# Eight of twelve groups of a modulation product moved from TensorE in the preparing stage to GpSimd in the gated linear stage

## The chip, the cores and the metric

The kernel runs on one core of one Trainium2 chip. The metric is the device time of one execution in microseconds (us). The engines are named as in the profile: PE (TensorE matmul) and PEld (its weight loads), DVE (VectorE), ACT (ScalarE), POOL (GpSimd), and SP (SyncE), which here only issues DMAs. Each engine works through its own instructions in their order, and waits on semaphores for the others.

## The reference, cut to what matters

The program is a mixer with two branches, a mixture of experts, and a second model of two layers. Only the modulation is touched. `c` and `c_ctx` are vectors of 1024, `w_mod` is 1024 x 6144, and each of the six parts is 1024 wide:

```python
mod_lat = split(silu(c) @ w_mod + b_mod, 6)         # sh1, sc1, g1, sh2, sc2, g2
mod_ctx = split(silu(c_ctx) @ w_mod + b_mod, 6)     # only csh1, csc1 are used: need_ctx is false
h_lat = rms_norm(x, norm_mix_g) * (1 + sc1) + sh1   # before the mixer
h_ctx = rms_norm(ctx, norm_mix_g) * (1 + csc1) + csh1
x = x + g1 * token_mixer(h_lat, h_ctx)              # delta-rule branch, gated linear branch, merge
h = rms_norm(x, norm_ffn_g) * (1 + sc2) + sh2       # before the experts
x = x + g2 * moe_ffn(h)
```

So `sh1` and `sc1` are wanted for both vectors before the mixer, and `g1, sh2, sc2, g2` for `c` alone, from the end of the merge on. All data are float32.

## The kernel before

The code is written out engine by engine, in stages (`stage`, line 156) that end with a barrier of all engines. `build` calls `prepare`, `gdn` (the delta-rule branch, 134.9 to 700 us), `gla` (the gated linear branch), `merge`, `experts` and `second`, each a row of such stages.

**prepare** computes the modulation and the first norm. The 6144 columns go in 12 groups of 512, each a 2 MB load (`load_group`) into one of four slots. Per group, PE multiplies `cs` (silu of both vectors, two columns) with the group's eight row tiles (L505), DVE copies the 2 x 512 result out of its bank (L522), PE turns it to columns with four small matmuls one group later (L495), and DVE adds the bias into `modT` (L526). `modT` has 48 columns of 128 for each vector: 0 to 15 are `sh1, sc1` (groups 0 to 3), 16 to 47 the other four parts (groups 4 to 11). In between DVE makes the inverse root (L545), scales the tokens (L550, behind group 3), makes `gain` (L553, L555, in group 4) and writes `hT` in eight steps of two instructions (L533, in groups 5 to 8). The stage ends with the last L526. The next stage reads `hT` and `wba`.

**gla** has a first stage, in which SP issues the weights `wh` of heads 0 and 1 (`load_head`, 3 MB each) and PE makes the low-rank gate (L1232), and a main stage (L1248 on) with four heads. Head 0 is projected alone: PE runs `project(0, 0..7)`, `inside(0)`, `project(0, 8)`, and DVE `decay(0, 0..7)`. Then for each head there are eight steps `i`. In step `i` PE makes the state update (L1340), for `i >= 4` the outputs (L1352, L1354), and `project(h + 1, i)`; DVE makes `state(h, i)` (L1462, L1470) and then `decay(h + 1, i)`, and parts of `norm(h - 1)`. What PE takes from DVE in the order of the program:

- the outputs of step `i` wait for `state(h, i - 1)`, which stands on DVE behind `decay(h + 1, i - 2)`;
- `project(h + 1, 7)` waits for `value(h + 1, 0)` (L1450), the end of `decay` part 5;
- `inside(h + 1)` (L1308, L1313) waits for the third product (L1436) of part 6 for each direction.

Most of the DVE instructions of `decay` read two tensors in SBUF: L1378, L1393, the two scans L1401, L1407, L1410, six subtractions L1422 to L1424, eight products L1436; L1380, L1387 and L1395 read and write SBUF with one tensor. `state` and the copies L1384, L1389, L1450 read one operand in PSUM. SP issues head `h + 2` when both matmuls of part 7 and 8 of head `h` are done (`rb_mm`, L1261). POOL has no instruction in `gla`. PE's last work there is `squares(3)` (L1321), DVE's the last part of `norm(3)` (to L1498). **merge** reads columns 16 to 23 of `modT` at L1674.

## Time and profile before

| | us |
|---|---|
| median of 3 runs | 3244.03 (3236.37 to 3245.56) |
| the profiled execution, device time | 3235.3 |
| its span, first to last instruction | 3233.5 |
| PE busy in the span | 3010.9 (93%) |
| DVE busy | 2097.6 (65%) |
| ACT busy | 1608.9 (50%) |
| POOL busy | 143.7 (4%) |
| second part of prepare (L505 on) | about 27.7 to 134.9 |
| main stage of gla | 723.6 to 969.7 |

Device time and span differ by 1.8 us. A time in a row is counted from the start of the span. A matmul of float32 leaves two records on PE and two on PEld, so `x64` in a row of PE is 32 matmuls. In the diff and in the order rows, the line numbers of the changed kernel are its own.

### The profile page before, as it was taken

The page shows a single profiled execution, that of the slowest core. Times are in us where ns is not written, and L with a number is a line of the kernel's source. Part 1 is how long each engine was busy: PE and PEld are TensorE (multiplying, and loading weights), DVE is VectorE, ACT ScalarE, POOL GpSimd, SP SyncE. Part 2 cuts the span into 40 slices and gives each one's busy share as a digit, 9 for nine tenths or more (in the row PEclk, how much of TensorE's full clock was granted, in tenths as well). Part 3 has the DMA queues.
Part 4 walks back from the last instruction along what each step waited for, and adds up shares of the span by engine and source line. Part 5 has one row for each costly group of instructions (what it writes and reads, how often), then busy time and mean ns, then how long its engine had stood idle before and what let it go on. Part 6 is the DMA issues. An engine that isn't in the chain of part 4 may idle for free. (4 is left out here: it accounts for less than half of the span.)

```text
span 3233.5 us, 44597 instructions
## 1 busy us (share of the span) xinstructions
PE 3010.9 (93%) x17512; PEld 2454.1 (76%) x17513; DVE 2097.6 (65%) x3195; ACT 1608.9 (50%) x2237; POOL 143.7 (4%) x175
## 2 busy tenths in 40 slices
PE   7989999989989789999999999999697899997998
PEld 2458888857669767777777777777595799986998
DVE  2135555535546578998998998998474556574665
ACT  0024444422215277777777777776332435442453
POOL 0022233200000000000000000000000000000000
PEclk9899999999979889999999999999795799995999
DMA  7551110021106579999999999996450255540453
GB/s 263 157 93 28 33 40 7 1 81 39 40 1 200 179 297 361 364 357 362 365 358 360 365 363 355 363 368 241 136 146 11 60 166 174 150 124 1 137 183 124
DMA packets 257563, 602.58 MB, mean 186 GB/s; under 512 B 25954, under 2 KB 82505, under 8 KB 257225
## 3 DMA queue, kind: packets, MB, share of 16 engines
q1 hardware_dynamic: 256268, 599.25, 54.2%
q8 instruction: 142, 2.33, 0.3%
q14 instruction: 68, 0.56, 0.1%
q10 hardware_dynamic: 1085, 0.45, 0.1%
HBM read 595.24 MB, written 4.39 MB: 185 GB/s over the span
## 5 line engine op out<-in xcount | busy, mean ns | idle before, releaser
L2000 DVE TENSOR_TENSOR moe_raw_r<-moe_raw,moe_hi 128x2048 fp32r<-128x2048 f32 x320 | 720.6, 2286 | 36.9 <-ACT moe_hi L1939 36.9
L1939 ACT ACTIVATE moe_hi<-moe_raw 128x2048 fp32r<-128x2048 f32 x320 | 599.3, 1906 | 0.0
L2722 PE MATMUL banks<-xs_r,w_hi 128*128 128x272 f32 (+1 forms) x1632 | 475.5, 291 | 25.2 <-DVE w_raw_r L3144 16.6
L2726 PE MATMUL banks<-xs_r,w_raw_r 128*128 128x272 f32 (+1 forms) x1632 | 472.8, 290 | 0.0
L2723 PE MATMUL banks<-xs_r,w_hi 128*128 128x272 f32 (+1 forms) x1632 | 470.2, 288 | 0.0
L1835 PE MATMUL banks<-moe_raw_r,moe_xs 128*128 128x512 f32 x1024 | 387.1, 435 | 0.0
L2966 ACT ACTIVATE w_hi<-w_raw 128x512 fp32r<-128x512 f32 (+1 forms) x416 | 256.9, 619 | 245.2 <-PE banks L2726 202.2
L2722 PEld LDWEIGHTS banks<-xs_r,w_hi 128*128 128x128 f32 x1632 | 311.3, 191 | 30.4 <-issue 22.4
L2726 PEld LDWEIGHTS banks<-xs_r,w_raw_r 128*128 128x128 f32 x1632 | 311.3, 191 | 2.9
L2723 PEld LDWEIGHTS banks<-xs_r,w_hi 128*128 128x128 f32 x1632 | 311.8, 191 | 0.2
L3144 DVE TENSOR_TENSOR w_raw_r<-w_raw,w_hi 128x512 fp32r<-128x512 f32 (+1 forms) x416 | 271.5, 676 | 56.9 <-ACT w_hi L2966 52.8
L1835 PE MATMUL banks<-moe_hi,moe_xs 128*128 128x512 f32 x772 | 296.4, 439 | 12.3 <-DVE moe_raw_r L2000 10.5
L1835 PEld LDWEIGHTS banks<-moe_raw_r,moe_xs 128*128 128x128 f32 x1024 | 193.8, 189 | 34.4
L1871 PEld LDWEIGHTS banks<-con,gu_tok 128*128 128x128 f32 x1024 | 190.9, 191 | 28.9 <-ACT gu_tok L1947 8.6
L791 PE MATMUL banks<-hT,wq 128*128 128x256 f32 (+1 forms) x512 | 180.3, 495 | 4.1 <-PEq L163 1.6
L1835 PE MATMUL banks<-moe_hi,y_tok_r 128*128 128x512 f32 x508 | 170.8, 418 | 5.3 <-DVE gu L2010 3.0
L1835 PEld LDWEIGHTS banks<-moe_hi,moe_xs 128*128 128x128 f32 x772 | 141.4, 190 | 45.2 <-issue 23.6
L1871 PE MATMUL banks<-con,gu_tok 128*128 128x64 f32 x1024 | 170.1, 250 | 1.1 <-ACT gu_tok L1947 1.1
L1835 PE MATMUL banks<-moe_raw_r,y_tok_r 128*128 128x512 f32 x512 | 162.0, 398 | 0.0
L2000 DVE TENSOR_TENSOR moe_raw_r<-moe_raw,moe_yT_r 128x2048 fp32r<-128x2048 f32 x64 | 146.3, 2286 | 0.0
L1050 DVE COPY_PREDICATED Tt<-gcon,banks 128x512 f32<-128x512 uint32 x112 | 81.1, 732 | 93.1 <-PE banks L838 68.1
L1880 PE MATMUL banks<-y_tok,pickT 128*128 128x512 f32 x256 | 139.7, 631 | 1.2 <-ACT y_tok L1958 1.2
(474 smaller groups left out, 5305.1 us busy)
## 6 DMA issues: line engine op xcount, KB each, us to landing
moe_raw<-in_w_gu SPq DMA_DIRECT2D x256, 1024.0 KB, 8.2
moe_raw<-in_w_down SPq DMA_DIRECT2D x128, 1024.0 KB, 10.2
w_raw<-in_w_ff SPq DMA_DIRECT2D x256, 256.0 KB, 3.0
w_raw<-in_w_in SPq DMA_DIRECT2D x112, 256.0 KB, 2.7
ring_mod<-in_w_mod SPq DMA_DIRECT2D x12, 2048.0 KB, 8.2
wq<-in_w_in SPq DMA_DIRECT2D x32, 512.0 KB, 4.3
wh<-in_w_in SPq DMA_DIRECT2D x8, 1024.0 KB, 9.5
mg_raw<-in_w_in SPq DMA_DIRECT2D x32, 256.0 KB, 3.0
```

What stands on the lines that cost most here:

```text
L791: ins = pe.matmul(out, wq[:, h % 2, n, k, :], hT[:, k, lo:TOK], start=(k == 0), stop=(k == KT - 1))
L1050: dve.copy_predicated(Tt[:, d, :, :], level_mask(d, lv), tiled(ps[4 + d][:, :])).then_inc(tt_v, 1)
L1835: ins = pe.matmul(ps[pair(e) + c][:, :], x[:, k, :], w[:, k * D + c * 512:k * D + c * 512 + 512], start=(q == 0 and i < 2), stop=(q == 3 a ...
L1871: ins = pe.matmul(ps[pair(e) + h][:, i * SLOTS:(i + 1) * SLOTS], gs[:, s, (4 * h + m) * P:(4 * h + m + 1) * P], fold, start=True, stop=True)
L1880: ins = pe.matmul(ps[4 + i][:, :], pickTs[e % 2][:, t * P:(t + 1) * P], y[:, c * 512:(c + 1) * 512], start=False, stop=(e == NEXP - 1))
L1939: act.activation(hi[n % HI_SLOTS][:, :], raw[n % UNITS][:, :], ACT.Copy).then_inc(his, 1)
L2000: dve.tensor_tensor(rest[n % UNITS][:, :], raw[n % UNITS][:, :], hi[n % HI_SLOTS][:, :].bitcast(F32), ALU.subtract).then_inc(los, 1)
L2722: pe.matmul(bank, w_hi, x[:, 0, 0:n_cols], start=first, stop=False)
L2723: pe.matmul(bank, w_hi, x[:, 1, 0:n_cols], start=False, stop=False)
L2726: ins = pe.matmul(bank, w_lo, x[:, 0, 0:n_cols], start=False, stop=last)
L2966: act.activation(hi[n % HI2][:, 0:w], raw[n % RING2][:, 0:w], ACT.Copy).then_inc(his, 1)
L3144: dve.tensor_tensor(rest[n % RING2][:, 0:w], raw[n % RING2][:, 0:w], hi[n % HI2][:, 0:w].bitcast(F32), ALU.subtract).then_inc(los, 1)
```

## The change

`prepare` keeps groups 0 to 3 and drops groups 4 to 11, with their loads, matmuls, turns and copies. DVE makes `gain` and all of `hT` at the end of the stage. `cs` now lives for the whole program.

`gla` gets the eight dropped groups, for `c` alone. A group is loaded in two halves of four row tiles (`load_mod`, 1 MB, 16 units in all) into two slots. POOL multiplies a half with the four columns of `cs` (128 x 2048), adds its two pairs (128 x 1024), and adds again (128 x 512); the second half has one more addition, to the first half's sum. That is 7 instructions for a group and 56 in all, each of which waits for the one before it. PE sums over the partitions at the stage's end with 32 matmuls of one column against `ones`, and one DVE instruction adds the bias. SP issues units 0 and 1 behind `wh` in the first stage; units 2 to 4 ahead of head 2, units 5 to 8 behind head 2, units 9 to 15 behind head 3, each when POOL is through with the unit two before it.

```diff
             @block.sync
             def _(sp):
-                for g in range(4, 12):
-                    sp.wait_ge(summed, g - 3)
-                    load_group(sp, g)
...
-                for g in range(12):
-                    pe.wait_ge(mod_in[g % 4], g // 4 * 16 + 16)
-                    if g >= 4:
-                        pe.wait_ge(copied, g - 3)
+                for g in range(4):
+                    pe.wait_ge(mod_in[g], 16)
...
-                    if g == 4:
-                        dve.wait_ge(taken, 4)
-                        dve.tensor_scalar(gain[:, :, :], modT[:, KT:2 * KT, :], 1.0, None, ALU.add).then_inc(gained, 1)
...
-                    if 5 <= g <= 8:
-                        shifted(2 * g - 10)
-                        shifted(2 * g - 9)
-                group_out(11)
+                group_out(3)
+                dve.wait_ge(taken, 4)
+                dve.tensor_scalar(gain[:, :, :], modT[:, KT:2 * KT, :], 1.0, None, ALU.add).then_inc(gained, 1)
...
+                for k in range(KT):
+                    shifted(k)
...
+        def load_mod(sp, u):
+            g, half = 4 + u // 2, u % 2
+            sp.dma_start(mod_ring[:, half], a["w_mod"][0][half * 4 * P:(half + 1) * 4 * P, g * 512:(g + 1) * 512]
+                         .rearrange("(k p) n -> p k n", p=P)).then_inc(mod_in[half], 16)
...
             @block.sync
             def _(sp):
+                def late(*units):
+                    for u in units:
+                        sp.wait_ge(mod_p, 7 * (u // 2 - 1) + (3, 7)[u % 2])
+                        load_mod(sp, u)
+
+                late(2, 3, 4)
                 for h in range(GLA_H - 2):
                     sp.wait_ge(rb_mm, 2 * h + 2)
                     load_head(sp, h + 2)
+                    late(*range(5 + 4 * h, 9 + 4 * h))
+                late(13, 14, 15)
+
+            @block.gpsimd
+            def _(pool):
+                for g in range(8):
+                    for half in range(2):
+                        w, n = mod_ring[:, half], 7 * g + 3 * half
+                        pool.wait_ge(mod_in[half], g * 16 + 16)
+                        pool.tensor_tensor(w, w, cs[:, 4 * half:4 * half + 4, 0:1].broadcast_to([P, 4, 512]), ALU.mult).then_inc(mod_p, 1)
+                        pool.wait_ge(mod_p, n + 1)
+                        pool.tensor_tensor(w[:, 0:2, :], w[:, 0:2, :], w[:, 2:4, :], ALU.add).then_inc(mod_p, 1)
+                        pool.wait_ge(mod_p, n + 2)
+                        if half == 0:
+                            pool.tensor_tensor(mod_sum[:, g, :], w[:, 0, :], w[:, 1, :], ALU.add).then_inc(mod_p, 1)
+                        else:
+                            pool.tensor_tensor(w[:, 0, :], w[:, 0, :], w[:, 1, :], ALU.add).then_inc(mod_p, 1)
+                            pool.wait_ge(mod_p, n + 3)
+                            pool.tensor_tensor(mod_sum[:, g, :], mod_sum[:, g, :], w[:, 0, :], ALU.add).then_inc(mod_p, 1)
...
                 squares(GLA_H - 1)
+                pe.wait_ge(mod_p, 7 * 8)
+                for m in range(4 * 8):
+                    ins = pe.matmul(ps[2][:, m:m + 1], mod_sum[:, m // 4, m % 4 * P:(m % 4 + 1) * P], ones[:, 0:1],
+                                    start=True, stop=True)
+                ins.then_inc(mod_mm, 1)
...
                 for part in range(3):
                     norm(GLA_H - 1, part)
+                dve.wait_ge(mod_mm, 1)
+                dve.tensor_tensor(modT[:, 2 * KT:6 * KT, 0], ps[2][:, 0:4 * KT], vec[:, V_BMOD + 2 * KT:V_BMOD + 6 * KT], ALU.add)
```

DVE in the second part of prepare, before, from the scaling of the tokens on:

```order
L550 TENSOR_TENSOR allT<-allT,rinv 128x512 x8
L522 COPY rows_mod<-banks 2x512
L526 TENSOR_TENSOR modT<-banks,vec 128x8
L553 TENSOR_SCALAR gain<-modT 128x16
L555 TENSOR_TENSOR gain<-gain,vec 128x16
L522 COPY rows_mod<-banks 2x512
L526 TENSOR_TENSOR modT<-banks,vec 128x8
L533 TENSOR_SCALAR hT<-allT,gain,modT 128x256 x4
```

and now, to the branch at the stage's end:

```order
L541 TENSOR_TENSOR allT<-allT,rinv 128x512 x8
L517 TENSOR_TENSOR modT<-banks,vec 128x8
L544 TENSOR_SCALAR gain<-modT 128x16
L546 TENSOR_TENSOR gain<-gain,vec 128x16
L524 TENSOR_SCALAR hT<-allT,gain,modT 128x256 x16
L161 UNCONDITIONAL_BRANCH
```

The 16 instructions that write `hT`, four of which went with each of four groups, now stand in one run behind the scaling.

POOL, before, at the end of its program (`vb`, `kbg`, `kd` are tiles of the delta-rule branch):

```order
L1159 TENSOR_TENSOR vb<-vtok,gates 128x512
L1162 TENSOR_TENSOR kbg<-ktok,gates 128x512 [waits gdn_k_v]
L1162 TENSOR_TENSOR kbg<-ktok,gates 128x512
L1166 TENSOR_TENSOR kd<-ktok,gates 128x512 [waits gdn_su_mm]
L1166 TENSOR_TENSOR kd<-ktok,gates 128x512
L777 UNCONDITIONAL_BRANCH
```

and now, from the same place on, through the first of the eight groups (`mod_ring` holds the loaded halves, `mod_sum` the sums):

```order
L1155 TENSOR_TENSOR kd<-ktok,gates 128x512
L766 UNCONDITIONAL_BRANCH
L1271 UNCONDITIONAL_BRANCH [waits barrier_Pool_Activation_PE_DVE_SP_gather]
L1277 TENSOR_TENSOR mod_ring<-mod_ring,cs 128x2048 [waits mod_late0]
L1279 TENSOR_TENSOR mod_ring<-mod_ring 128x1024 [waits gla_mod_p]
L1282 TENSOR_TENSOR mod_sum<-mod_ring 128x512 [waits gla_mod_p]
L1277 TENSOR_TENSOR mod_ring<-mod_ring,cs 128x2048 [waits mod_late1]
L1279 TENSOR_TENSOR mod_ring<-mod_ring 128x1024 [waits gla_mod_p]
L1284 TENSOR_TENSOR mod_ring<-mod_ring 128x512 [waits gla_mod_p]
L1286 TENSOR_TENSOR mod_sum<-mod_sum,mod_ring 128x512 [waits gla_mod_p]
```

Eight times these seven are added where POOL had nothing.

PE at the end of the main stage of gla, before:

```order
L1352 MATMUL banks<-le,lS 128x64 [waits gla_s1]
L1354 MATMUL banks<-latt,lv 128x64
L1321 MATMUL banks<-lsq,con 128x256 [waits gla_sq_v] x2
L161 UNCONDITIONAL_BRANCH
L176 UNCONDITIONAL_BRANCH [waits barrier_Pool_Activation_PE_DVE_SP_release]
```

and now:

```order
L1376 MATMUL banks<-le,lS 128x64
L1378 MATMUL banks<-latt,lv 128x64
L1345 MATMUL banks<-lsq,con 128x256 [waits gla_sq_v] x2
L1391 MATMUL banks<-con,mod_sum 128x1 [waits gla_mod_p]
L1391 MATMUL banks<-con,mod_sum 128x1 x31
L161 UNCONDITIONAL_BRANCH
```

The 32 matmuls stand between the last sum of squares and the barrier.

## Rows read from the trace of the kernel before

**Rows 1.** Stretches: length, busy us (records) by engine, PE clock, DMA share, GB/s.

```profile
703.00:723.60 20.60, 15.37 (x32) 3.20 (x32) 2.39 (x5) 0.00 (x0) 0.00 (x0) 0.84 1.00 280
723.60:969.70 246.10, 233.03 (x976) 167.61 (x976) 126.35 (x236) 50.31 (x79) 0.00 (x0) 0.89 0.10 29
```

**Rows 2.** Timeline, DVE in prepare: start us, us, engine line op, tiles, count.

```profile
69.02 4.91 DVE L550 TENSOR_TENSOR allT<-allT,rinv 128x512 f32<-128x512 f32 x8
...
133.33 0.17 DVE L526 TENSOR_TENSOR modT<-banks,vec 128x8 f32<-128x8 f32 x1 [0.74 <-PE banks L495]
```

**Rows 3.** DVE groups of prepare: busy us, mean ns of one, idle before.

```profile
L533 DVE TENSOR_SCALAR hT<-allT,gain,modT 128x256 f32<-128x256 f32 x16 | 5.5, 410 | 0.3 <-issue 0.3
```

**Rows 4.** POOL groups of the whole span, each form apart.

```profile
L1150 POOL TENSOR_TENSOR attd<-attd,gcon 128x512 f32<-128x512 f32 x8 | 10.5, 1313 | 48.1 <-ACT attd L928 48.1
L1159 POOL TENSOR_TENSOR vb<-vtok,gates 128x512 f32<-128x512 f32 x16 | 16.4, 1048 | 31.3 <-ACT vtok L977 31.3
L1156 POOL COPY Tt<-con 128x512 f32<-128x512 f32 x16 | 10.1, 638 | 188.2 <-PE banks L854 188.2
L476 POOL COPY xT<-allT 128x2048 f32<-128x2048 f32 x1 | 1.9, 1891 | 27.4 <-POOLq L163 27.4
```

**Rows 5.** Timeline, POOL and DVE in gdn, two places.

```profile
344.11 2.06 POOL L1159 TENSOR_TENSOR vb<-vtok,gates 128x512 f32<-128x512 f32 x2 [2.60 <-ACT vtok L977]
...
345.09 0.15 DVE L1097 TENSOR_SCALAR nstd<-nsum 128x2 f32<-128x2 f32 x1
345.16 1.02 DVE L1098 TENSOR_SCALAR nstd<-nsum 128x4 f32<-128x4 f32 x1
...
350.85 2.24 POOL L1162 TENSOR_TENSOR kbg<-ktok,gates 128x512 f32<-128x512 f32 x2 [4.69 <-DVE ktok L1109]
...
351.02 1.16 DVE L1115 TENSOR_TENSOR osc<-osb,nrin 128x256 f32<-128x256 f32 x1
```

**Rows 6.** Two DVE lines of gdn: count, ns minimum/median/maximum, first and last start.

```profile
L1115 DVE TENSOR_TENSOR osc<-osb,nrin x8: 415/1161/1164, 351.0 to 698.8; 128x256 f32<-128x256 f32 x8
...
L1076 DVE COPY vn<-banks x64: 291/292/296, 277.5 to 694.0; 128x128 f32<-128x128 f32 x64
```

**Rows 7.** Timeline, DVE in gla: head 0, then the steps of heads 0 and 1.

```profile
738.61 1.22 DVE L1393 TENSOR_TENSOR lz<-lz,lns 128x1024 f32<-128x1024 f32 x1
...
747.32 0.68 DVE L1450 COPY lv<-banks 128x512 f32<-128x512 f32 x1
...
776.43 1.22 DVE L1393 TENSOR_TENSOR lz<-lz,lns 128x1024 f32<-128x1024 f32 x1
...
798.10 0.48 DVE L1470 SCALAR_TENSOR_TENSOR lS<-lS,lgl,banks 128x256 f32<-128x256 f32 x1 [1.24 <-PE banks L1354]
...
834.44 1.22 DVE L1393 TENSOR_TENSOR lz<-lz,lns 128x1024 f32<-128x1024 f32 x1
...
859.40 0.42 DVE L1436 TENSOR_TENSOR le<-le,lqT 128x256 f32<-128x256 f32 x1
```

**Rows 8.** Timeline, PE in gla: what takes DVE's results there.

```profile
751.61 3.62 PE L1300 MATMUL banks<-hT,wh 128*128 128x256 f32 x16
...
803.14 0.33 PE L1352 MATMUL banks<-le,lS 128*128 128x64 f32 x2
...
867.52 1.04 PE L1308 MATMUL banks<-con,le 128*128 128x128 f32 x8
```

**Rows 9.** DVE's idle time before L1470 in 776 to 800, and in 834 to 860.

```profile
  PE banks L1354: 10.1, 6
...
  PE banks L1354: 6.8, 6
```

**Rows 10.** Timeline, the end of gla's main stage, PE and DVE.

```profile
961.21 2.08 PE L1321 MATMUL banks<-lsq,con 128*128 128x256 f32 x4 [1.96 <-DVE lsq L1484]
...
966.93 0.69 DVE L1498 TENSOR_TENSOR ybT<-loT,rb 128x512 f32<-128x512 f32 x1
```

**Rows 11.** The stretch of L659 and L660, matmuls of 8 columns, columns as in rows 1.

```profile
153.40:160.30 6.90, 6.86 (x33) 6.86 (x33) 0.09 (x1) 0.69 (x1) 0.00 (x0) 0.50 0.96 226
```

More of the change, by code:

```diff
@@ L360, in build @@
         metaT = sb("metaT", [P, KT, META])
+        cs = sb("cs", [P, KT, 2])
         rows_stored = ctx.enter_context(nc.semaphore("bias_rows_stored"))
@@ L366, in build @@
             wba = sb("wba", [P, KT, 32], mix)
-            prepare(nc, a, ps, con, vec, xT, modT, hT, wba, wba_in, ident, ones)
+            prepare(nc, a, ps, con, vec, xT, modT, cs, hT, wba, wba_in, ident, ones)
             yaT = sb("yaT", [P, GDN_H, LAT], mix)
@@ L370, in build @@
             ybT = sb("ybT", [P, KT, LAT], mix)
-            gla(nc, a, ps, con, vec, hT, ybT, ident, ones)
+            gla(nc, a, ps, con, vec, hT, ybT, modT, cs, ident, ones)
             merge(nc, a, ps, hT, yaT, ybT, xT, modT)
@@ L374, in build, with prepare @@
         second(nc, a, ps, con, vec, xT, metaT, rows_stored, ident, ones, out)
-def prepare(nc, a, ps, con, vec, xT, modT, hT, wba, wba_in, ident, ones):
+def prepare(nc, a, ps, con, vec, xT, modT, cs, hT, wba, wba_in, ident, ones):
     with contextlib.ExitStack() as ctx:
@@ L416, in load_group @@
         def load_group(sp, g):
-            sp.dma_start(ring[:, g % 4, :, :], a["w_mod"][0][:, g * 512:(g + 1) * 512].rearrange("(k p) n -> p k n", p=P))\
-                .then_inc(mod_in[g % 4], 16)
+            sp.dma_start(ring[:, g, :, :], a["w_mod"][0][:, g * 512:(g + 1) * 512].rearrange("(k p) n -> p k n", p=P))\
+                .then_inc(mod_in[g], 16)
         with stage(nc, "pre_rows pre_tok pre_con pre_t pre_e") as (block, rows_in, tok_in, con_in, turned, taken):
@@ L494, in turn @@
                     for m in range(4):
-                        ins = pe.matmul(ps[4 + g % 4][:, 2 * m:2 * m + 2], rows2[:, g % 4, m * P:(m + 1) * P], ident[0:2, 0:2],
+                        ins = pe.matmul(ps[4 + g][:, 2 * m:2 * m + 2], rows2[:, g, m * P:(m + 1) * P], ident[0:2, 0:2],
                                         start=True, stop=True)
@@ L499, in _ @@
                 pe.wait_ge(cs_in, 1)
-                for g in range(12):
-                    pe.wait_ge(mod_in[g % 4], g // 4 * 16 + 16)
-                    if g >= 4:
-                        pe.wait_ge(copied, g - 3)
+                for g in range(4):
+                    pe.wait_ge(mod_in[g], 16)
                     for k in range(KT):
-                        ins = pe.matmul(ps[g % 4][0:2, :], cs[:, k, :], ring[:, g % 4, k, :], start=(k == 0), stop=(k == KT - 1))
+                        ins = pe.matmul(ps[g][0:2, :], cs[:, k, :], ring[:, g, k, :], start=(k == 0), stop=(k == KT - 1))
                     ins.then_inc(summed, 1)
@@ L513, in _ @@
                         ins.then_inc(norm_sum, 1)
-                turn(11)
+                turn(3)
             @block.vector
@@ L534, in shifted @@
                                           modT[:, k, c:c + 1], ALU.mult, ALU.add)
-                for g in range(12):
+                for g in range(4):
                     group(g)
@@ L550, in _ @@
                             dve.tensor_tensor(allT[:, k, :], allT[:, k, :], rinv[:, :], ALU.mult).then_inc(scaled, 1)
-                    if g == 4:
-                        dve.wait_ge(taken, 4)
-                        dve.tensor_scalar(gain[:, :, :], modT[:, KT:2 * KT, :], 1.0, None, ALU.add).then_inc(gained, 1)
-                        dve.wait_ge(gained, 1)
-                        dve.tensor_tensor(gain[:, :, :], gain[:, :, :],
-                                          vec[:, V_MIX:V_MIX + KT].unsqueeze(2).broadcast_to([P, KT, 2]), ALU.mult).then_inc(gained, 1)
-                    if 5 <= g <= 8:
-                        shifted(2 * g - 10)
-                        shifted(2 * g - 9)
-                group_out(11)
+                group_out(3)
+                dve.wait_ge(taken, 4)
+                dve.tensor_scalar(gain[:, :, :], modT[:, KT:2 * KT, :], 1.0, None, ALU.add).then_inc(gained, 1)
+                dve.wait_ge(gained, 1)
+                dve.tensor_tensor(gain[:, :, :], gain[:, :, :],
+                                  vec[:, V_MIX:V_MIX + KT].unsqueeze(2).broadcast_to([P, KT, 2]), ALU.mult).then_inc(gained, 1)
+                for k in range(KT):
+                    shifted(k)
 def gdn(nc, a, ps, con, vec, hT, yaT, metaT, wba, wba_in, rows_stored, ident, ones):
@@ L1174, with gla @@
 CONV_OPS = 3 * 9 + 2 * 3
-def gla(nc, a, ps, con, vec, hT, ybT, ident, ones):
+def gla(nc, a, ps, con, vec, hT, ybT, modT, cs, ident, ones):
     w_in = a["w_in"]
@@ L1211, in gla @@
         loaded = [ctx.enter_context(nc.semaphore(f"gla_w{p}")) for p in range(2)]
+        mod_ring = sb("mod_ring", [P, 2, KT // 2, 512])
+        mod_sum = sb("mod_sum", [P, 8, 512])
+        mod_in = [ctx.enter_context(nc.semaphore(f"mod_late{p}")) for p in range(2)]
+        def load_mod(sp, u):
+            g, half = 4 + u // 2, u % 2
+            sp.dma_start(mod_ring[:, half], a["w_mod"][0][half * 4 * P:(half + 1) * 4 * P, g * 512:(g + 1) * 512]
+                         .rearrange("(k p) n -> p k n", p=P)).then_inc(mod_in[half], 16)
         def load_head(sp, h):
@@ L1225, in _ @@
                 load_head(sp, 1)
+                load_mod(sp, 0)
+                load_mod(sp, 1)
             @block.tensor
@@ L1254, in gla @@
                  cum_v, v_v, diff_v, e_v, kd_v, att_v, s0, s1, o_v, sq_v, var_v, inv_v,
-                 n_v, y_v, exp_a, ln_a, ex_a, silu_a, std_a):
+                 n_v, y_v, exp_a, ln_a, ex_a, silu_a, std_a, mod_p, mod_mm):
             ups, ss = (up0, up1), (s0, s1)
```

10 lines of the change are left out of this document (3 added, 7 removed).

## The prediction

> **What bounds the kernel now.** I read the stretches first, then the places that the change touches. In the main stage of gla PE is busy 233.0 of 246.1 us and DVE 126.4, and POOL has nothing there [rows 1]. So PE sets the time, DVE has slack at each place where PE takes something from it, and POOL and DMA (share 0.10) stand free. In prepare DVE's scaling of the tokens ends at 69.02 + 4.91 = 73.9, and the last instruction of the stage, the bias of group 11, at 133.33 + 0.17 = 133.5 [rows 2]. Between them PE works through groups 4 to 11, and only 5.5 us of DVE work on `hT` is wanted by the next stage [rows 3]. All sums are made against the profiled execution, 3235.3 us; the median of the runs shown lies 8.7 higher, and I add what comes out to the median.
>
> **Prepare: -53.5 us.** Turn 3 is through on PE before the scaling ends on DVE. Behind the 73.9 come the bias of group 3 and two `gain` instructions, 3 x 0.2 (as the last row of [rows 2], with a handover), and the 16 instructions of `hT`, 5.5 us [rows 3]: 80.0. The stage ends 133.5 - 80.0 = 53.5 us sooner. The 16 MB of loads that go from here lay beside PE. PE now idles some 10 us while DVE ends; its next matmuls may start at half clock, which I price with the same effect below.
>
> **The first stage of gla: +2 us.** SP issues two more loads of 1 MB before it can reach the barrier. The DMA engines are full there (share 1.00 at 280 GB/s [rows 1]), so the two take 7.5 us to move, and SP may wait for room in the queue for none or all of that. I take 2; ends 0 and 7.5.
>
> **POOL's work: 127 us.** A two-input instruction of 512 columns takes 1.3 us with two full operands and 1.05 with one broadcast operand, as the multiplication by `cs` has; copies of 512 and 2048 columns take 0.64 and 1.89, so about 0.2 of each is a start [rows 4]. The multiplication (2048) is then 4 x 1.05 less three starts, 3.6; the first addition (1024) 2.4; a 512 addition 1.3. 16 x 3.6 + 16 x 2.4 + 24 x 1.3 = 127, without saved starts 139. There are 246 us for it, so POOL alone isn't late. The Trainium skill, GPSIMD Engine Reference, section 3.1, gives 4.5 us for a float32 addition of 2048 columns on GpSimd; with that for the 16 multiplications POOL would work 14 us longer, and the total would move up by at most as much.
>
> **What POOL does to DVE: +74 us.** In gdn both engines work at once, and that is the nearest row. L1115 reads two SBUF tensors and takes 0.42 us alone, 1.16 in six of eight [rows 6]; in those it starts just behind a POOL multiplication at 350.85 and ends when that is through [rows 5]. At 345.16 a DVE instruction of four columns takes 1.02 us, the length of the POOL instruction (the second of two from 344.11) that it meets [rows 5]. The short one just ahead of it, 0.15 us, got through between the two POOL instructions. A DVE instruction that reads PSUM isn't touched: L1076 has a maximum of 0.296 us in 64, many beside POOL [rows 6]. So a DVE instruction with two SBUF inputs, or one that goes from SBUF to SBUF, waits for the end of the POOL instruction that runs, and the next one waits for the next POOL instruction. The Trainium skill, SBUF — State Buffer, section Who interferes with whom, extends this to every DVE instruction with two SBUF inputs, the scans too, which no row here shows, and says nothing on turns; without the two scans a head, some 15 us of the term would be open. In gla such instructions stand in runs (`decay` parts 3 to 6), and a run gives POOL a turn between any two. The delay of a run is then the POOL work that falls in it, less the time DVE would have waited for PE anyway, less DVE work on PSUM that runs beside POOL, less PE's slack. How much POOL work there is follows from SP's order: units 0 to 4 before head 0 is projected, 5 to 8 behind the load of head 2, 9 to 15 behind the load of head 3.
>
> Head 0: unit 0 is through before the run starts at 738.6 [rows 7]. Units 1 to 4 are 4 x 7.3 + 2 x 1.3 = 31.8 us in 14 instructions, 1 us of it done by then. The run to `value` (L1450, 747.32) has 15 instructions that wait [rows 7], so nearly all 30.6 us land there. PE takes it at 751.6, with 3.6 us of slack [rows 7, 8]: +27.
>
> The steps of head 0 (counted as before): units 5 and 6 land behind 4 MB, 14 us at 280 GB/s [rows 1], at 774.5, and the run starts at 776.4 [rows 7]. Of units 5 to 8, again 31.8 us, 29.9 remain. DVE waited 10.1 us for PE there [rows 9], and 2.8 us are on PSUM. The update that stood at 798.1 comes at 815, and PE wants it at 803.1 [rows 7, 8]: +12.
>
> The steps of head 1: units 9 to 15, 7 x 7.3 + 4 x 1.3 = 56.3 us, from 829 on; at 834.4 some 51 are left [rows 7]. DVE's waits are 6.8 us [rows 9], its work beside POOL 5 (six L1470, a reciprocal, L1450). The products end at 859.8 + 51 - 12 = 899 instead of 859.8, and PE's second direction wants its own at 868.0 [rows 7, 8]: +30. Then POOL is through, and heads 2 and 3 run as before.
>
> Three long waits of PE, and the one in prepare, each let its clock fall: 16 matmul records of 3.6 us at full clock [rows 8] can cost up to 3.6 more at half clock; 1.5 each for the three in gla, 5 in all. 27 + 12 + 30 + 5 = 74. Ends: 0 if nothing meets, and 139 + 14, all POOL work and four full clock losses.
>
> **The tail of gla: +9.8 us.** 32 matmuls of one column, 64 records, stand behind L1321, which ends at 963.3 [rows 10]. Matmuls of 8 columns took 6.86 us for 33 records at half clock [rows 11], 0.21 each: 13.6 us, to 976.9, and DVE's addition to 977.4, where it ended at 967.6 [rows 10]. That half clock holds here too is likely: gdn's had it behind other thin matmuls. Ends: at full clock half, +3; with dearer weight loads 0.31 each, +16. By the Trainium skill, TensorE: Matmul & The Clock Gate, section LDWEIGHTS, a load of 128 columns takes 107 ns, which would make the 64 records 6.8 us and the term +3. SP's order costs nothing: head 3's load waits for unit 8's slot, free some 20 us before `rb_mm`.
>
> **Sum.** -53.5 + 2 + 74 + 9.8 = +32, so 3267 against the profiled execution and 3276 against the median. A clear loss: what moved off PE lands on DVE's waits.
>
> **The rivals.** (1) *DVE keeps its turn.* If DVE, once it has waited, keeps its place through a run, each run waits once, 3.6 us at most; the slack takes nearly all, some 3 us remain. -53.5 + 2 + 3 + 9.8 = -39: 3205, faster. For it: POOL waits for its own semaphore between two instructions, and DVE could slip ahead. Against: the long wait at 345.16, right behind another instruction that got through [rows 5]. Chance 0.15. (2) *Two short ones per turn.* If two DVE instructions of 0.4 us pass between two POOL instructions, as L1097 did [rows 5], fewer POOL instructions fall ahead of what PE wants: some 4 + 7 + 15 us less of the 74, so +6: 3250. Chance 0.12. (3) *The forecast*, slower: decided by POOL work in DVE's runs; below about 42 us of delay the kernel would not be slower. Chance 0.60. (4) *POOL dearer*, through handovers between its dependent instructions or slower instructions (139 us): units meet DVE longer, and some reach head 2; +15 on the forecast: 3291, up to 3305. Chance 0.09. The last 0.04 are for a wait that holds for a few of the DVE lines only, with times around 3230.
>
> **How the numbers follow.** The likeliest is the forecast, 3276. Its own range is 3260 to 3292, from the ends of POOL's work (127 to 139), of the tail and of the first stage. The range for 8 in 10 leaves rival 1 out and takes in rivals 2 and 4: 3240 to 3302. A difference of 0.3% (about 10 us) is what a measurement can tell from none: faster by more 0.17 (rival 1 and half of the rest), within it 0.12 (most of rival 2), slower 0.71.
>
> **What would show it.** In the changed profile: prepare's last DVE instruction near 80; the mean of the DVE lines L1393, L1401, L1407, L1422 to L1424 and L1436 of before well over theirs, while `state` and the PSUM copies keep theirs; PE idle some 27 us before head 0's part 7, some 12 and 30 us in the steps of heads 0 and 1, none in heads 2 and 3; POOL busy 125 to 140 us in gla, in three stretches; 64 records of 0.2 us at the end. It is wrong if those DVE lines keep their means (rival 1), if POOL's multiplications take over 4.2 us, or if PE stays busy although DVE waits.

## The result, and the profile of the changed kernel

The changed kernel takes 3251.4 us (median of 12 runs, 3246.9 to 3257.1) where the kernel before takes 3234.7 (12 runs beside them, 3229.9 to 3245.6). The ratio is 1.0049, with a 95% interval of 1.0039 to 1.0059: slower, by some 16 us (16.7 between the medians). The span of the profiled execution went from 3233.5 to 3251.5 us. So the sign of the forecast was right and its size was not: +32 us were forecast, and about half of that came.

Three stretches of the changed kernel hold the places in gla that the sum spoke of: its first stage, its main stage to the last sum of squares, and from there to merge's first matmul. The rows give, for each stretch, busy time with instruction count per engine, the granted clock of TensorE, the busy share of the DMA engines and GB/s. The first is a view of the changed kernel:

```profile
653.43:671.94 18.51, 16.86 (x33) 3.41 (x33) 1.36 (x2) 0.04 (x1) 0.00 (x0) 0.84 1.11 324
671.94:973.36 301.42, 246.83 (x972) 177.25 (x972) 215.80 (x231) 50.18 (x78) 142.92 (x56) 0.83 0.24 78
973.36:995.53 22.17, 15.52 (x69) 15.11 (x69) 5.49 (x10) 3.62 (x7) 0.00 (x0) 0.50 0.13 39
```

The second is the same work in the kernel before:

```profile
706.67:723.69 17.02, 15.37 (x33) 3.23 (x33) 1.36 (x2) 0.04 (x1) 0.00 (x0) 0.91 1.11 326
723.69:961.21 237.52, 230.96 (x973) 166.41 (x973) 122.32 (x231) 49.85 (x78) 0.00 (x0) 0.91 0.10 30
961.21:974.04 12.83, 2.07 (x4) 1.20 (x5) 5.29 (x9) 3.61 (x7) 0.00 (x0) 0.50 0.23 69
```

Read the second row of each together. PE does the same work, and the stage is 63.9 us longer. DVE's 231 instructions are the same too, and their busy time rose from 122.3 to 215.8 us: they did nothing more, they were held. The other rows give -53.2 us up to gla (706.67 to 653.43), +1.5 for the first stage and +9.3 for the tail.

The last row of DVE's timeline in prepare, where [rows 2] had its last instruction at 133.33:

```profile
75.41 5.25 DVE L524 TENSOR_SCALAR hT<-allT,gain,modT 128x256 f32<-128x256 f32 x16
```

It ends at 80.66 (forecast 80.0). POOL's multiplications in gla (line, engine, operation, names, shapes, count, busy us, mean ns, and the idle time before them):

```profile
L1277 POOL TENSOR_TENSOR mod_ring<-mod_ring,cs 128x2048 f32<-128x2048 f32 x16 | 63.2, 3951 | 133.1 <-DMA mod_ring<-in_w_mod 133.1
```

The multiplications have a mean of 3.95 us and a minimum of 3.60; the first additions 2.60 and 2.35, the additions of 512 columns 1.6 and 1.3 (2.35 and 1.32 stand in the timeline below). POOL waits for DVE just as DVE waits for POOL. How the two take turns is seen in the timeline of head 0's projection, the place of [rows 7]. Columns are start, duration, engine, line:

```profile
688.17 2.35 POOL L1279 TENSOR_TENSOR mod_ring<-mod_ring 128x1024 f32<-128x1024 f32 x1
688.39 3.21 DVE L1422 TENSOR_TENSOR lz<-lz,lns 128x1024 f32<-128x1024 f32 x1
690.59 2.13 POOL L1284 TENSOR_TENSOR mod_ring<-mod_ring 128x512 f32<-128x512 f32 x1
691.63 1.64 DVE L1424 TENSOR_SCALAR lz<-lz 128x1024 f32<-128x1024 f32 x1
...
708.06 2.40 POOL L1279 TENSOR_TENSOR mod_ring<-mod_ring 128x1024 f32<-128x1024 f32 x1
708.19 2.56 DVE L1452 TENSOR_TENSOR le<-cum 128x256 f32<-128x256 f32 x1
710.54 1.32 POOL L1284 TENSOR_TENSOR mod_ring<-mod_ring 128x512 f32<-128x512 f32 x1
710.66 1.75 DVE L1453 TENSOR_TENSOR le<-cum 128x512 f32<-128x512 f32 x1
...
713.47 0.41 DVE L1451 TENSOR_TENSOR le<-cum 128x256 f32<-128x256 f32 x1
713.49 3.85 POOL L1277 TENSOR_TENSOR mod_ring<-mod_ring,cs 128x2048 f32<-128x2048 f32 x1
713.81 3.82 DVE L1452 TENSOR_TENSOR le<-cum 128x256 f32<-128x256 f32 x1
...
721.44 0.68 DVE L1479 COPY lv<-banks 128x512 f32<-128x512 f32 x1
```

Nearly every DVE instruction whose inputs are all in SBUF starts just behind a POOL instruction and ends with it plus its own work: at 708.19 a subtraction of 0.42 us takes 2.56, because the addition of 708.06 runs until 710.46. Then POOL has its turn again. At 713.47 one instruction slips in between two of POOL's, as the short one of [rows 5] had. `value` (L1479) reads PSUM and is not touched. PE takes it at 722.17. PE's waits for DVE in the main stage, from the view of waits (what waited, for what, total us, times, the longest):

```profile
PE banks L1376 <- DVE lS L1499: 21.6, 5, 8.5
PE banks L1324 <- DVE lv L1479: 20.6, 1, 20.6
PE banks L1332 <- DVE le L1465: 5.8, 1, 5.8
```

All three are the places of the forecast: part 7 of head 0's projection, the outputs that want `state` in the steps of heads 0 and 1, and `inside(2)`. The tail is one row of PE's timeline, where [rows 10] had nothing:

```profile
975.23 13.65 PE L1391 MATMUL banks<-con,mod_sum 128*128 128x1 f32 x64
```

### The profile page after: what moved, and what is told of

It reads as the page before. It is cut to its first block and busy times, and to the rows that moved or that the text cites. A ratio compares the mean times of both kernels' runs of the same rounds, so it can differ in the third digit from the quotient of the medians.

```text
span 3251.5 us, 44370 instructions
## 1 busy us (share of the span) xinstructions
PE 2973.7 (91%) x17384; PEld 2459.4 (76%) x17385; DVE 2183.5 (67%) x3180; ACT 1609.1 (49%) x2237; POOL 286.4 (9%) x231
## 5 line engine op out<-in xcount | busy, mean ns | idle before, releaser
L2753 PE MATMUL banks<-xs_r,w_hi 128*128 128x272 f32 (+1 forms) x1632 | 474.4, 291 | 25.3 <-DVE w_raw_r L3175 16.7
```

The costliest lines, as they stand in the source:

```text
L2753: pe.matmul(bank, w_hi, x[:, 0, 0:n_cols], start=first, stop=False)
```

## The experiments

The theory was the forecast's: a POOL instruction holds off a DVE instruction that reads SBUF, and the two engines take turns, instruction by instruction. The rivals were that the loads or SP's order did it, that DVE loses what POOL is busy however it is cut, and that the tail and prepare do not add up. All ratios are against the kernel before, run beside it on the same chip; where there is none, the reading is the profile's. "Main stage" is from head 0's gate to the last sum of squares, 237.5 us in the kernel before.

### No arithmetic on POOL

```diff
+                pool.memset(mod_sum[:, :, :], 0.0).then_inc(mod_p, 1)
...
                         pool.wait_ge(mod_in[half], g * 16 + 16)
-                        pool.tensor_tensor(w, w, cs[...].broadcast_to([P, 4, 512]), ALU.mult).then_inc(mod_p, 1)
...
+                        pool.sem_inc(mod_p, 3 + half - (g + half == 0))
```

> The changed kernel with its loads, their order and the 32 matmuls of one column, but without GpSimd's arithmetic: GpSimd sets mod_sum to zero once (one instruction of 4096 columns at the start of the stage) and then only takes the arrival of each unit and frees its slot. The sums of groups 4 to 11 are left out, so the gates and the second norm's modulation hold the bias alone. Theory A (POOL's instructions hold DVE's off): all waits of PE for DVE in the three places go (20.6; 0.95 and 8.5; 4.9, 6.8 and 5.8 us), 64 to 66 us less than the changed kernel: about -42 us against the kernel before, ratio 0.987. Theory B (loads or SP's order hold DVE or PE up): the waits stay in part; over 20 of the 64 us would still be there, ratio above 0.993. The tail stays at +9.3 us and the first stage at +1.5 in both.

Ratio 0.9867 (0.9844 to 0.9890). The stretches of this kernel, first stage, main stage, tail:

```profile
652.62:671.07 18.45, 16.80 (x32) 3.39 (x33) 1.35 (x2) 0.04 (x1) 0.04 (x1) 0.84 1.12 331
671.07:910.09 239.02, 232.53 (x972) 167.00 (x973) 122.32 (x231) 49.91 (x78) 3.47 (x1) 0.90 0.28 98
910.09:932.35 22.26, 15.53 (x69) 15.11 (x69) 5.50 (x10) 3.62 (x7) 0.00 (x0) 0.50 0.14 41
```

The same 16 MB come in, and the main stage is 239.0 us: 62.4 less than the changed kernel's 301.4, and DVE's busy time is back at 122.3. The loads and SP's order cost nothing there. What held DVE is POOL's arithmetic; the theory stands, the rival of the loads falls.

### Prepare alone

```diff
-                load_mod(sp, 0)
-                load_mod(sp, 1)
...
-                pe.wait_ge(mod_p, 7 * 8)
-                for m in range(4 * 8):
-                    ins = pe.matmul(ps[2][:, m:m + 1], mod_sum[...], ones[:, 0:1], start=True, stop=True)
```

> Only the change in prepare: four groups there, and nothing of the late groups anywhere (no loads, no arithmetic, no 32 matmuls; one DVE copy of the bias stands for them, so the gates and the second norm's modulation are left out but for the bias). Both theories: prepare 53 us shorter, ratio 0.9835. Set against the run without GpSimd's arithmetic it prices the loads in gla's first stage and the tail together: 10.8 us if the two stage differences add up (1.5 and 9.3), 0 to 4 if part of the tail is hidden behind something that would wait anyway.

Ratio 0.9816 (0.9794 to 0.9838), some 60 us less; its main stage is 237.48 us and the stretch from the last sum of squares to merge 12.89. Against the run above, the tail is 22.26 - 12.89 = 9.4 us, nothing of it hidden. Between the two the first stage and the main stage differ by 1.6 and 1.5 us, which is not the loads, as a later section shows.

### POOL's work cut into pieces of 256 and of 512 columns

```diff
+                def many(n_cols, op, out, x, y):
+                    for at in range(0, n_cols, 256):
+                        ins = pool.tensor_tensor(out[:, at:at + 256], x[:, at:at + 256], y(at), op)
+                    ins.then_inc(mod_p, 1)
...
-                        pool.tensor_tensor(w, w, cs[...].broadcast_to([P, 4, 512]), ALU.mult).then_inc(mod_p, 1)
+                        many(2048, ALU.mult, w, w, lambda at: cs[...].broadcast_to([P, 256]))
```

> The changed kernel with each GpSimd instruction cut to pieces of 256 columns (8, 4, 2 and 2 pieces in place of one), arithmetic and order the same. A piece should take 0.6 us (multiplication) or 0.75 (addition), 163 us in all by a start of 0.2 us each, against 127. Theory A1 (turns, one instruction of each engine in alternation): a DVE instruction waits for a piece at most, so a run of 15 loses some 10 us, not 27; PE's three places lose 20 to 25 us together instead of 64, and the kernel is near -20 us against before, ratio 0.992 to 0.995. Theory A2 (DVE loses what POOL is busy, however it is cut): delay in proportion to POOL's busy time, 73 us in place of 64, and work left over for head 2: +30 us, ratio 1.009.

> The changed kernel with GpSimd's instructions cut to pieces of 512 columns (4, 2, 1 and 1), as a third length between the whole ones and 256 columns, which made gla's main stage 62 and 10 us longer than no arithmetic. Theory A1 (a wait of a piece less its start at each turn): a piece of 512 holds DVE off for about 1.0 us against 0.45 and 2.5, so 22 to 30 us, about -12 to -20 us against before. Rival (the gain of the short pieces came from something else, as from dropping the handover between dependent instructions, which pieces of one instruction do not have): 10 to 15 us, as with 256.

With 256 columns the ratio is 0.9904 (0.9882 to 0.9926), with 512 the one time is 3216.6 us. The main stages, of 256 and then of 512:

```profile
668.63:917.82 249.19, 237.70 (x972) 170.94 (x972) 154.58 (x231) 50.18 (x78) 185.85 (x240) 0.88 0.30 96
...
669.33:937.07 267.74, 242.45 (x973) 173.27 (x973) 183.85 (x231) 50.19 (x78) 159.29 (x120) 0.87 0.27 88
```

and the subtraction of 256 columns (L1452 above), first with pieces of 256, then of 512 (minimum, median and maximum in ns):

```profile
L1458 DVE TENSOR_TENSOR le<-cum x8: 413/830/946, 692.0 to 864.7; 128x256 f32<-128x256 f32 x8
...
L1458 DVE TENSOR_TENSOR le<-cum x8: 419/1259/1490, 699.1 to 883.6; 128x256 f32<-128x256 f32 x8
```

POOL is busy longer the finer it is cut (143, 159, 186 us), and the stage gets shorter: 62.4 us over the run without arithmetic for whole instructions, 28.7 for 512, and 11.7 for 256 (this one over the kernel before, whose clock in gla's first stage it shares; the reason stands below). So DVE does not lose POOL's busy time; it loses one instruction of POOL at each turn, and the length of the piece is the price. The forecast for 512 was 22 to 30. For 256 I expected 20 to 25 and 11.7 came: I had counted the holds on DVE, and part of these falls in time in which DVE would have waited for PE. DVE's busy time shows it: it rose by 32.3, 61.5 and 93.5 us for 256, 512 and whole instructions, and the stage by 11.7, 28.7 and 62.4, so 21 to 33 us of holds never reached PE. Of the 11.7 us only 5 are waits of PE; the other 6.7 are PE's own busy time at the same work (237.70 against 230.96), at a mean clock of 0.88 and not 0.91.

### The same groups on DVE

```diff
+                def modulate(*units):
+                    for u in units:
+                        ...
+                        for k in range(4):
+                            ...
+                            dve.scalar_tensor_tensor(mod_sum[:, g, :], w, c, mod_sum[:, g, :], ALU.mult, ALU.add).then_inc(mod_p, 1)
...
                         value(h, 1)
+                        modulate(*((), (5, 6), (10, 11), (15,))[h])
...
                             decay(h + 1, i)
+                            if i < 3:
+                                modulate(2 + 5 * h + i)
```

> The same groups 4 to 11 in gla, but on DVE instead of GpSimd: one multiply-add of 512 columns for each 128 rows of w_mod (64 instructions, some 0.6 us each, 38 us in all), two units in the projection of head 0, and for each of heads 0 to 2 one unit at the end of steps 0, 1 and 2 and two in the place where DVE waits 6 to 10 us for PE's transposes; a ring of three units of 1 MB. Theory A (what costs is the other engine's turns, not the work): 38 us fit in the 120 us in which DVE waits for PE, about 5 us of them reach PE; -53.2 + 1.5 + 5 + 9.3 = -37 us against before, ratio 0.9885. Rival: DVE has no slack where the units stand (every step of PE waits for a state of DVE), and half of the 38 us or more reach PE: ratio 0.993 or more.

Ratio 0.9851 (0.9828 to 0.9874). Its main stage (its tail is 22.23 us, as above):

```profile
669.05:908.07 239.02, 232.54 (x973) 167.00 (x973) 165.47 (x295) 49.90 (x78) 0.00 (x0) 0.90 0.30 98
```

DVE does 64 instructions and 43.1 us more (0.75 us for each of the 56 multiply-adds of 512 columns, where I had put 0.6; 0.48 for the 8 plain multiplications), and the main stage is as long as with no arithmetic at all. The rival (no slack where the units stand) falls. DVE is busy 43 us more and PE sees none of it, since the work stands where DVE waits for PE; in the changed kernel DVE is busy 93.5 us more, at places that nobody chose, and PE sees 62. The two are not the same amount of work: a multiply-add does in one pass what takes a multiplication and an addition on POOL, 43 us against 126.

### The 32 matmuls of one column spread

```diff
+                        if h and i == 0:
+                            pe.wait_ge(att_v, 2 * h + 1)
+                            late(*((0, 5), (5, 10), (10, 18))[h - 1])
...
-                for m in range(4 * 8):
+                late(23, 32).then_inc(mod_mm, 1)
```

> The version with groups 4 to 11 on DVE, and the 32 matmuls of one column no longer all at the end of gla: 5 behind the first part of head 2's projection, 5 behind that of head 3's, 8 behind the first step of head 3, 5 ahead of its sum of squares, where PE waits 1.2, 1.2, 2.2 and 2.0 us for DVE, and 9 at the end. Theory A (the tail costs because nothing else stands beside it; a matmul of one column takes 0.214 us at full clock and 0.43 at half): the first 23 fit in PE's waits, and the last 9 (3.9 us) in the 4.4 us in which DVE ends the norm of head 3: the tail falls from +9.3 to about +1, so 8 us less than with the 32 at the end, ratio 0.9825 against before. Rival: PE's waits are only shown where the chain over DVE leaves them, and work put there delays that chain: each of the 23 costs its own length, 5 to 7 us, and the gain is 2 to 3 us, ratio 0.984 to 0.985.

3181.5 us, ratio 0.9828 (0.9809 to 0.9847). The main stage and the tail of this kernel, and ten records of its spread matmuls:

```profile
672.89:907.60 234.71, 234.51 (x1018) 170.38 (x1019) 165.32 (x295) 49.84 (x78) 0.00 (x0) 0.92 0.31 101
907.60:920.57 12.97, 5.69 (x24) 5.27 (x24) 5.29 (x10) 3.62 (x7) 0.00 (x0) 0.50 0.23 72
...
821.39 1.27 PE L1328 MATMUL banks<-con,mod_sum 128*128 128x1 f32 x10
```

The tail is 12.97 us, 0.1 more than in the kernel before, and the 23 matmuls that went into the main stage did not make it longer. PE's waits of 1.2 and 2.2 us are filled (234.51 busy of 234.71). Theory A holds: the ratio alone would not tell it from the rival's 0.984, the two rows do. This is the fastest version that does all the work, 58 us under the kernel before by the medians of its call (3239.6), and faster than the changed kernel. Prepare alone, with none of the late work, had 0.9816. Its main stage is even 4.3 us shorter than the one above; 3.2 of that lie before `inside(0)`, where the clock was 1.00 and not 0.90, and are no merit of the change.

### What it is in a POOL instruction that holds DVE

Three runs put other instructions on 4096, 2600 and 1400 columns in the place of POOL's arithmetic (memsets, copies, multiplications by a constant), meant to be about as long; they leave the sums of groups 4 to 11 out. A fourth made the multiplications with one tensor input and kept the sums. The first three differ from the changed kernel as here:

```diff
-                        pool.tensor_tensor(w, w, cs[...], ALU.mult).then_inc(mod_p, 1)
+                            pool.memset(flat[:, 0:cols], 0.0).then_inc(mod_p, 1)
...
+                            pool.tensor_copy(flat[:, 0:cols], flat[:, 0:cols]).then_inc(mod_p, 1)
...
+                            pool.tensor_scalar(flat[:, 0:cols], flat[:, 0:cols], 0.5, None, ALU.mult).then_inc(mod_p, 1)
```

> The changed kernel with each of GpSimd's instructions replaced by one that only writes zeros for about as long: 4096 columns for the multiplication (3.5 us), 2600 and 1400 for the additions (2.3 and 1.3), with the same waits, loads and tail; the sums of groups 4 to 11 are left out. Theory A1 (a GpSimd instruction holds DVE off by its reading of SBUF): no delay in gla's main stage, waits of 0 to 3 us, near -42 us against before. Theory A3 (any GpSimd instruction on SBUF holds DVE off, a write too): the same 60 to 64 us as with the arithmetic, +16 to +20 us against before.

> The changed kernel with each multiplication made of four instructions of 512 columns with one tensor input and a scalar of each partition (0.64 us each by the copy of that size in the preparing stage), and the additions in pieces of 512 columns with two tensor inputs (1.3 us). Theory A (both kinds hold DVE off for their length less a start of 0.2 us): gla's main stage longer by 15 to 22 us than without the arithmetic. Rival (only instructions with two tensor inputs hold DVE off): DVE instructions beside the multiplications keep their free times, and the stage is longer by 8 to 12 us.

> As the run with memsets, but each of GpSimd's instructions is a copy of mod_sum onto itself (4096, 2600 and 1400 columns, some 3.6, 2.3 and 1.4 us by the copy of 2048 columns in 1.89 us): one read and one write of SBUF, no arithmetic on groups 4 to 11, whose sums are left out. Theory A1 (reading decides: a GpSimd instruction that reads SBUF holds off DVE's instructions with two SBUF inputs): the subtraction of 256 columns has a median of 2 us or more, as beside the arithmetic (3.2), and gla's main stage is 50 to 65 us longer than without arithmetic. Rival (two tensor inputs decide on both sides: DVE's second input shares a way with GpSimd's second input only, as the run with one-input multiplications suggests): the subtraction stays at 0.42, only DVE's instructions with one SBUF input wait, and the stage is 0 to 8 us longer, as with memsets (0).

> As the run with copies, but each GpSimd instruction is a multiplication of mod_sum by the constant 0.5 (one tensor input, no scalar read from SBUF); the sums of groups 4 to 11 are left out. Theory A1: as with copies, 50 to 65 us. Rival: 0 to 8 us with DVE's two-input instructions free. Of the 0.37 us by which DVE's one-input instruction of 1024 columns was longer beside a multiplication with a scalar in SBUF: if it came from the reading of the scalar, DVE's one-input instructions here wait either the whole length (as beside memsets) or not at all; if from the form of instruction, they wait 0.4 us again.

Each of these four has one time: 3197.6 us with memsets, 3268.9 with copies, 3376.3 with the constant, 3204.9 with one-input multiplications. What follows rests on their profiles. With memsets the main stage is 237.54 us, that of the kernel before (237.52), with POOL busy 125.4 us in it. A part of its timeline (POOL's one row stands for six instructions in a row):

```profile
683.22 13.94 POOL L1281 MEMSET mod_sum<- 128x1400 f32 x6
...
686.73 1.22 DVE L1417 TENSOR_TENSOR lz<-lz,lns 128x1024 f32<-128x1024 f32 x1
...
688.71 2.34 DVE L1425 TENSOR_TENSOR_SCAN cum<-keep,lz 128x512 f32<-128x512 f32 x2
691.08 1.14 DVE L1429 COPY ltot<-cum 128x8 f32<-128x8 f32 x1
692.26 0.69 DVE L1431 TENSOR_TENSOR cum<-ltot,cum 128x512 f32<-128x512 f32 x1
```

Instructions with two SBUF inputs and the scans run free beside a memset (1.22, two scans in 2.34, 0.69), while the copy of 8 columns, 0.16 us by itself, takes 1.14. (Some two-input instructions have longer records there too, up to 3.4 us; they stand right behind a held copy and end with it.) With copies that read SBUF the picture is that of the arithmetic again:

```profile
672.64:979.78 307.14, 251.35 (x972) 180.85 (x972) 217.71 (x231) 50.19 (x78) 142.85 (x56) 0.82 0.24 77
```

The main stage is 69.6 us longer than before, with POOL busy 142.9 us, as with the arithmetic (the forecast was 50 to 65); the median of the subtraction of 256 columns is 2.07 us. So reading decides, not the number of inputs: theory A1 holds, and the rival formed from the one-input multiplications falls. The Trainium skill, SBUF — State Buffer, section Who interferes with whom, says that an instruction with two SBUF inputs on DVE contends only with a GpSimd instruction that reads SBUF, and one from SBUF to SBUF in a two-port mode with any; these two runs agree, with 0 and 69.6 us.

The two runs with `tensor_scalar` on POOL need a closer look. With one-input multiplications of 512 columns the stage is 248.36 us, +10.9, inside what the rival had expected and under theory A's 15 to 22. Each took 1.56 us, not the 0.64 that I had taken from a copy, and a DVE instruction beside one was held 0.4 us in most cases (the fast one of 1024 columns 1.06 us, 0.69 alone): it came free 1.0 us before the multiplication's end. With the constant and 4096 columns:

```profile
L1285 POOL TENSOR_SCALAR mod_sum<-mod_sum 128x4096 f32<-128x4096 f32 x16 | 171.3, 10705 | 24.6 <-DMA mod_ring<-in_w_mod 22.3 <-POOL mod_sum L1285 2.3
...
723.08 10.56 POOL L1285 TENSOR_SCALAR mod_sum<-mod_sum 128x4096 f32<-128x4096 f32 x1 [0.15 <-POOL mod_sum L1285]
723.15 9.03 DVE L1450 TENSOR_TENSOR le<-cum 128x256 f32<-128x256 f32 x1
```

it is 10.7 us for 4096 columns, three times a copy's 3.6, and POOL is busy 375.7 us. The stage is 189 us longer, which is neither theory's number, since both were made for 143 us of POOL work; but it is 0.50 us for each us of POOL's, and the copies' 69.6 is 0.49 of 142.9. The turns are there too. The subtraction at 723.15, 0.41 us alone, was held 8.6 us, until 1.9 us before POOL's instruction ended, and the next two DVE instructions slipped through in what was left of it. That is why the other subtraction line has a median of 0.41 us and a maximum of 3.3 there: it shows who slips through, not how long a hold is. Beside 2600 and 1400 columns a two-input instruction was held until 1.1 and 0.8 us before the end; a copy of 8 columns was held to the end (6.55 us beside one of 6.94). By the expectation that would put the short holds of the run before down to the scalar that it reads from SBUF; but the lengths differ too (1.56 us against 3.7 and more), so this is not shown. So `tensor_scalar` holds DVE's two-input instructions for most of its length when it is long, and for little of it at 512 columns. Theory A1 stands in both runs, less this early release, whose reason stays open. In the words of the same section of the Trainium skill, the engine that issues first has the shared ports for the whole instruction: beside copies and `tensor_tensor` the rows agree (the subtraction of 708.19 ends 0.3 us behind POOL's addition), beside `tensor_scalar` they show the release 0.8 to 1.9 us before the end, and the rows decide.

## Why the forecast was right in its sign and wrong in its size

**Prepare, -53.5:** -53.2. Right.

**First stage, +2:** +1.5, for another reason. SP is not what ends it. In the first 8 us of the stage, with the loads in flight, the changed kernel had a clock of 0.63 and 12 matmul records, and the run with pieces of 256 columns, which has the same loads, 0.82 and 16, as the kernel before (in this order):

```profile
653.43:661.43 8.00, 8.00 (x12) 1.54 (x13) 0.00 (x0) 0.00 (x0) 0.00 (x0) 0.63 1.08 318
...
651.64:659.64 8.00, 8.00 (x16) 1.74 (x17) 0.00 (x0) 0.00 (x0) 0.00 (x0) 0.82 1.11 321
...
706.70:714.70 8.00, 8.00 (x16) 1.72 (x17) 0.00 (x0) 0.00 (x0) 0.00 (x0) 0.82 1.11 327
```

PE comes out of a 7 us wait for DMA there, and how long it then stays at half clock differs from kernel to kernel: four of the eleven profiled changed kernels have 18.4 to 18.5 us, seven 16.9 to 17.4. Of the four, the two in which POOL holds nothing up also take 1.5 us more in head 0's projection, 32.9 against 31.4.

**POOL's work, 127 us:** the free lengths are 3.60, 2.35 and 1.3 us, which make 126. Right. Of the 143 us in the profile the rest is POOL's own waiting for DVE.

**What POOL does to DVE, +74:** +63.9. This is the term that was mis-sized, by 10 us, and its parts are off in both directions. The parts of the main stage, changed kernel, to `inside(0)`, to `inside(1)`, to `inside(2)`, its rest, and heads 2 and 3:

```profile
671.94:728.43 56.49, 35.88 (x116) 25.70 (x117) 47.13 (x32) 10.49 (x16) 44.51 (x17) 0.73 0.29 98
728.43:797.05 68.62, 59.16 (x241) 42.14 (x240) 50.56 (x50) 11.31 (x18) 36.26 (x14) 0.88 0.34 108
797.05:872.89 75.84, 62.98 (x246) 45.09 (x245) 63.15 (x55) 13.01 (x20) 54.93 (x22) 0.84 0.43 139
872.89:887.46 14.57, 8.78 (x38) 7.13 (x36) 10.22 (x9) 0.89 (x3) 7.22 (x4) 0.77 0.00 1
887.46:973.36 85.90, 80.03 (x338) 57.18 (x336) 44.74 (x86) 14.47 (x22) 0.00 (x0) 0.86 0.00 1
```

The same parts of the kernel before:

```profile
723.69:755.06 31.37, 31.29 (x116) 23.15 (x117) 18.15 (x32) 10.38 (x16) 0.00 (x0) 0.95 0.07 23
755.06:809.50 54.44, 54.44 (x241) 38.97 (x240) 25.97 (x50) 11.20 (x18) 0.00 (x0) 0.97 0.20 59
809.50:867.52 58.02, 56.85 (x246) 40.81 (x245) 31.39 (x59) 12.90 (x20) 0.00 (x0) 0.94 0.19 55
867.52:873.47 5.95, 5.95 (x38) 4.92 (x36) 1.97 (x4) 0.90 (x3) 0.00 (x0) 1.00 0.01 1
873.47:961.21 87.74, 82.42 (x339) 58.56 (x337) 44.84 (x86) 14.47 (x22) 0.00 (x0) 0.83 0.00 1
```

The length of a part less PE's busy time is PE's waiting, and the rise of PE's busy time at the same work is the clock:

| | forecast: wait, clock | measured: wait, clock | sum |
|---|---|---|---|
| projection of head 0 | 27, 1.5 | 20.5, 4.6 | 25.1 |
| steps of head 0 | 12, 1.5 | 9.5, 4.7 | 14.2 |
| steps of head 1 | 30, 1.5 | 17.5, 9.0 | 26.4 |
| heads 2 and 3 | 0, 0 | 0.5, -2.4 | -1.8 |
| main stage | 69, 5 | 48, 16 | 63.9 |

By part, 28.5 us were forecast and 25.1 came, then 13.5 and 14.2, then 31.5 and 26.4, then 0 and -1.8. The split of each into two columns is less firm than its sum: where DVE sets the time, a slower PE waits for it less.

*The waits* were put at 69 and were 48. The step that failed is "nearly all 30.6 us land there": I let POOL's work start with DVE's run and counted only what lay between. In the projection of head 0 the run from L1422 to `value` grew from 8.7 us (738.61 to 747.32, [rows 7]) to 33.1 (688.39 to 721.44), by 24.3 and not by some 30: unit 1's multiplication (684.49 to 688.09) had been done while DVE still waited 4.4 us for PE, and two DVE instructions slipped through free. In the steps of head 1 the stretch from L1422 to the last product grew from 25.4 us (834.44 to 859.82 before) to 58.8 (821.87 to 880.63), by 33.4 and not by 39: of the 51 us of POOL's work, 17.6 and not 12 fell beside DVE's waits for PE, its work on PSUM, or instructions that slipped through. That is the direction of my second rival (two short ones per turn), though its mechanism, two instructions at each turn, is not what the timeline shows: in head 0's run it is two in fifteen. *The clock* was put at 5 and was 16: I took 1.5 us for each of three waits, and head 1 alone had three (4.9, 6.8 and 5.8 us). PE's rows behind two of the waits:

```profile
722.17 6.43 PE L1324 MATMUL banks<-hT,wh 128*128 128x256 f32 x16 [20.61 <-DVE lv L1479]
...
786.20 0.69 PE L1376 MATMUL banks<-le,lS 128*128 128x64 f32 x2 [8.51 <-DVE lS L1499]
...
791.14 6.08 PE L1324 MATMUL banks<-hT,wh 128*128 128x256 f32 x16
```

The 16 records behind the 20.6 us took 6.43 us, at a granted clock of 0.56, where they took 3.62 at full clock [rows 8]: 2.8 more. The other 1.5 of that part's 4.6 come from the stage's start. Behind the 8.5 us the outputs and `project(1, 7)` took 10.9 us (786.20 to 797.05, clock 0.50 and then 0.59) where the kernel before took 6.4 (803.14 to 809.50): 4.5 more.

**The tail, +9.8:** +9.3, and 64 records in 13.65 us are 0.213 each, as taken from [rows 11]. Right. By the Trainium skill, TensorE: Matmul & The Clock Gate, section LDWEIGHTS, a load of 128 columns takes 107 ns; the record here is twice that at a granted clock of 0.50, and ten of them beside other work at full clock took 1.27 us, 0.127 each. So the Trainium skill's price is near what the rows show at full clock, and the +3 that I had worked out from it did not come because the clock stood at 0.50 here.

**Sum:** -53.2 + 1.5 + 63.9 + 9.3 = +21.5 at merge's first matmul (974.04 to 995.53), against +32. So 10 of the some 16 us by which the forecast was too high lie in the main stage, and 3.5 behind merge's first matmul: they come back over 2260 us of unchanged work, most of them in the second model. The times of the kernel before range over 16 us by themselves, and I have no cause for the 3.5. Without them the change would have been +21.5 us, two thirds of the forecast. In absolute numbers the forecast of 3276 lay 25 us over the measured 3251: 9 of these are the median of before, which was 3244.0 in the three runs shown and 3234.7 in twelve, and 16 the change.

**The rivals.** That DVE keeps its turn fell in the first look at the timeline. POOL dearer: no. That the kernel would be slower only above some 42 us of delay is right as an account: 63.9 came.

## What to carry to other kernels

Before work moves to GpSimd, look at what DVE does beside it: if DVE works through runs of SBUF-only instructions that TensorE waits for, each of them can cost up to one whole GpSimd instruction that reads SBUF, so the length of a GpSimd instruction matters more than the sum (62 us for instructions of up to 2048 columns, 12 for pieces of 256, with more POOL time in all). Ask first whether the waiting engine can do the work in its own waits: the same products and sums as 64 instructions on DVE, in places chosen for them, did not make the stage longer. A string of thin matmuls at the end of a stage stood alone at half clock here (13.65 us); spread over TensorE's short waits it cost next to nothing (a tail of 12.97 us against 12.83).

## What the runs showed of the hardware that I had not expected

- A `tensor_scalar` on POOL is slow for float32: 1.56 us for 512 columns and 10.7 for 4096, against 3.6 for a copy of 4096 and 3.5 for a memset. It lets DVE's two-input instructions go 0.8 to 1.9 us before its end: held 8.6 us beside one of 10.56, 0.4 beside one of 1.56.
- A memset on POOL does not touch DVE's instructions with two SBUF inputs (0.69 us for 512 columns beside it), but a DVE copy of 8 columns waits for it (1.14 us).
- The hold is mutual: POOL's multiplications had a mean of 3.95 us and a free length of 3.60.
- PE's clock after a wait: the 16 records behind a wait of 20.6 us took 6.43 us and not 3.62, at a granted clock of 0.56.
